# Prompt attention: VectorE makes sortable keys one beat later, and GpSimd takes the threshold step of each counting pass of the larger tiles

## What is computed

```python
def indexer_scores(iq, iw, ik):
    dots = jnp.einsum('nqhd,nsd->nqhs', iq, ik).astype(jnp.float32) * IDX_HEAD_DIM ** -0.5
    return jnp.einsum('nqh,nqhs->nqs', iw.astype(jnp.float32), jax.nn.relu(dots))
...
    def block(args):
        qb, iqb, iwb, qpos = args
        scores = indexer_scores(iqb, iwb, ik)
        scores = jnp.where((key_pos[None, :] <= qpos[:, None])[None], scores, -jnp.inf)
        _, idx = lax.top_k(scores, n_sel)
        valid = idx <= qpos[None, :, None]
        return selected_attention(qb, gather_rows(k, idx), gather_rows(v, idx), valid)
```

## Time and profile before

| what | value |
|---|---|
| median of three runs | 7764.09 us |
| profiled execution | 7772.33 us |
| span of its instructions | 7770.6 us |
| mean granted TensorE clock | 0.912 of full speed |
| PE busy over the span | 6543.4 us (84%) |
| DVE busy | 4540.9 us (58%) |
| ACT busy | 4234.9 us (54%) |
| POOL busy | 868.5 us (11%) |

### The profile page before, as it was taken

The page is one execution under the profiler, slowest core; times in us unless marked ns, Lnnn a source line. Parts: engine busy times, 40 slices in busy tenths (PEclk is TensorE's granted clock), DMA queues, the critical chain, the costliest instruction groups (busy, mean ns, idle before and its releaser), DMA issues. The chain is left out here.

```text
span 7770.6 us, 107932 instructions
## 1 busy us (share of the span) xinstructions
PE 6543.4 (84%) x37238; PEld 4012.5 (52%) x37238; DVE 4540.9 (58%) x12417; ACT 4234.9 (54%) x6108; POOL 868.5 (11%) x1398
## 2 busy tenths in 40 slices
PE   7999997888889998999989888847999469999970
PEld 2888884334444444444444444436455356666650
DVE  1555555777778877888888777853466400000017
ACT  1555553677778877888888887512333112221125
POOL 0111110000000000000000000000111233333335
PEclk9999998888989988999999999967999789999995
DMA  5121110000000000000000000023333168888888
GB/s 201 44 46 45 45 41 18 11 8 6 6 4 6 4 4 4 4 4 6 4 5 6 6 6 8 9 93 148 100 100 104 48 242 329 321 329 319 327 302 309
DMA packets 298319, 703.88 MB, mean 91 GB/s; under 512 B 120277, under 2 KB 166357, under 8 KB 257140
## 3 DMA queue, kind: packets, MB, share of 16 engines
q0 software_dynamic: 71520, 432.08, 15.0%
q1 hardware_dynamic: 225264, 257.29, 10.3%
q10 hardware_dynamic: 1094, 8.85, 0.3%
HBM read 559.43 MB, written 138.83 MB: 90 GB/s over the span
## 5 line engine op out<-in xcount | busy, mean ns | idle before, releaser
L818 ACT ACTIVATE at_junk<-at_key,at_thr 128x1024 int8<-128x1024 int16 (+56 forms) x858 | 1225.0, 1428 | 366.1 <-DVE at_thr L1061 322.3
L1018 DVE TENSOR_SCALAR_CACHE_REDUCE at_junk<-at_key,at_thr 128x384 int8<-128x384 f32 (+51 forms) x990 | 1301.8, 1315 | 46.1 <-issue 0.8
L906 PE MATMUL at_pS<-keep_KT,at_q 64*128 64x512 f32 (+3 forms) x2304 | 653.2, 645 | 200.9 <-DVE at_mx L1100 199.9
L1100 DVE CUSTOM_DVE_ANT_0 at_sm<-at_pS,at_drop 128x512 f32<-128x512 f32 (+3 forms) x1152 | 697.5, 643 | 87.5 <-PE at_pS L906 85.1
L937 PEld LDWEIGHTS at_pT<-keep_ident,at_sm 128*128 128x128 f32 x4224 | 505.7, 152 | 451.7 <-issue 433.0
L962 PE MATMUL at_pD<-keep_KT,keep_ident 128*128 128x512 f32 (+29 forms) x1602 | 653.5, 533 | 64.2 <-ACT at_relu L842 63.3
L917 PE MATMUL at_pD<-keep_IKT,at_iq 32*128 32x512 f32 (+3 forms) x2272 | 663.0, 662 | 35.4 <-ACT at_relu L842 34.3
L867 ACT ACTIVATE at_pt_sb<-at_pT 128x1024 f32<-128x1024 f32 (+3 forms) x576 | 546.1, 948 | 212.7 <-PE at_pT L937 211.7
L937 PE MATMUL at_pT<-keep_ident,at_sm 128*128 128x128 f32 x4224 | 641.1, 298 | 19.8 <-issue 11.5
L842 ACT ACTIVATE at_relu<-at_pD 128x1024 f32<-128x1024 f32 (+3 forms) x568 | 538.5, 948 | 203.2 <-PE at_pD L917 201.7
L2112 DVE TENSOR_TENSOR ex_gu<-ex_pg,ex_sg 128x256 f32<-128x256 f32 x98 | 41.6, 424 | 1003.3 <-ACT ex_sg L2094 1003.3
(11 more groups left out here) (432 smaller groups left out, 10134.9 us busy)
## 6 DMA issues: line engine op xcount, KB each, us to landing
scratch_ys<-ex_y SPq DMA_DIRECT2D x98, 512.0 KB, 2.7
scratch_x<-mx_x SPq DMA_DIRECT2D x33, 512.0 KB, 6.5
scratch_h<-mx_h SPq DMA_DIRECT2D x33, 512.0 KB, 2.6
cb_x<-scratch_x SPq DMA_DIRECT2D x33, 512.0 KB, 5.5
pj_x<-in_x_prompt SPq DMA_DIRECT2D x32, 512.0 KB, 3.6
mx_x<-in_x_prompt SPq DMA_DIRECT2D x32, 512.0 KB, 5.9
out_y_prompt<-cb_out SPq DMA_DIRECT2D x32, 512.0 KB, 4.6
scratch_qT<-pj_qT SPq DMA_DIRECT2D x33, 384.0 KB, 2.5
```

What stands on the lines that cost most here:

```text
L818: e.activation(junk[:, at], src[:, at], ACT.Sign, bias=bias, scale=-1.0, accum_out=cA[:, :]).then_inc(s["cnt"], 1)
L906: last = e.matmul(pS[:, kv, 0:w], Q[rows, t % 2, p, :], KT[rows, c * CUT:c * CUT + w], start=True, stop=True)
L1018: ch.then(e.tensor_scalar(junk[:, at], src[:, at], value, None, ALU.is_ge, ALU.add, accum_out=cD[:, :]))
L1100: e.tensor_tensor_reduce(sm[:, kv, at:at + w], pS[:, kv, 0:w], drop[:, t % 2, c * CUT:c * CUT + w], -HD ** -0.5, -NEG, ALU.add, ALU.min, m ...
```

## The change

Three things change in `phase_attend`.

1. `fresh_keys` is due one beat later than before, under the name `fresh`; ACT's `raw_scores` stays where it was.
2. For tiles with `CH(t) >= 4` (`guided`, L(t) from 1664 to 4096 keys: 20 tiles, 660 passes) the threshold step runs on GpSimd. DVE's count raises a semaphore `found`, ACT's count raises `cnt` as before, and GpSimd does kk, dlt and thr as three `tensor_scalar` instructions of 128x1 elements. kk is issued as soon as ACT's count is there, dlt waits for `found`. DVE goes from its count straight to the reads. The smaller tiles keep `decide` on DVE. `at_bigw` moves into the walk over the beats, at the end of the stage before.
3. The planner reckons 0.2 us instead of 0.7 us for a guided pass on DVE, and the load of the keys with `fresh`. This changes `splits`: over the 660 guided passes DVE counts 1,057,216 columns instead of 881,952, of 1,900,800. It changes `fills` too: over stages 8 to 27 from 201,265 to 161,427 columns.

```diff
+        guided = lambda t: CH(t) >= 4
+        found = lambda t, i: 33 * sum(guided(x) for x in range(2, t)) + i
+        needed = lambda t: sum(guided(x) for x in range(2, t + 1))
...
                 elif q == 0 and c > 0:
                     due(b, "wsum", (k, c - 1, 1))
                     due(b + 1, "raw", (k, c - 1))
+                    due(b + 2, "fresh", (k, c - 1))
...
+            if k + 1 < PT:
+                due(base + B - 1, "heads", k + 1)
...
-            v += 0.7 * len(passes)
+            v += sum(0.2 if guided(t) else 0.7 for t, i in passes)
...
+                def decide(t, i):
+                    n_act = L(t) - splits[t, i]
+                    e.wait_ge(s["cnt"], counted(t, i + 1 if i < 16 else i + 2))
+                    ch.ready()
...
+                    step = float(1 << (15 - i % 16))
+                    ch.link(e.tensor_scalar(kk[:, :], cA[:, :], 0.5, (2 * TOPK - 0.5 - n_act) / 2, ALU.mult, ALU.add))
+                    e.wait_ge(s["found"], found(t, i) + 1)
+                    ch.link(e.tensor_scalar(dlt[:, :], cD[:, :], kk[:, :], step, ALU.is_ge, ALU.mult))
+                    moved = e.tensor_scalar(thr[:, :], dlt[:, :], thr[:, :], -max(step / 2, 1.0), ALU.add, ALU.add)
+                    if i % 16 < 15:
+                        moved.then_inc(s["thr"], 1)
...
+                head_weights(2)
+                for beat in beats:
+                    for one in beat.get("heads", []):
+                        head_weights(one)
+                    for t, what, i in beat.get("find", []):
+                        if what == "pass" and guided(t):
+                            decide(t, i)
...
                 def count(t, i, src, value, n):
                     e.wait_ge(s["thr"], event(t, n))
                     ch.ready()
+                    wait(e, s["found"], found(t, i) if guided(t) else found(t, 0))
                     at = slice(0, splits[t, i])
-                    ch.then(e.tensor_scalar(junk[:, at], src[:, at], value, None, ALU.is_ge, ALU.add, accum_out=cD[:, :]))
+                    done = e.tensor_scalar(junk[:, at], src[:, at], value, None, ALU.is_ge, ALU.add, accum_out=cD[:, :])
+                    if guided(t):
+                        done.then_inc(s["found"], 1)
+                    else:
+                        ch.then(done)
...
                         if i == 0:
                             ch.ready()
                             wait(e, s["thr"], event(t, 0))
+                            wait(e, s["found"], found(t, 0))
+                            wait(e, s["cnt"], counted(t, 0))
+                            wait(e, s["needed"], needed(t - 1))
...
-                    for one in beat.get("raw", []):
+                    for one in beat.get("fresh", []):
                         fresh_keys(*one)
...
-                        early = what == "pass" and VECTOR * splits[t, i] > SCALAR * (L(t) - splits[t, i])
+                        early = what == "pass" and not guided(t) and VECTOR * splits[t, i] > SCALAR * (L(t) - splits[t, i])
...
-                        if what == "pass" and not early:
+                        if what == "pass" and not guided(t) and not early:
                             decide(t, i)
```

More of the change, by code:

```diff
@@ L657, in phase_attend @@
         pD = pb("at_pD", [P, 2, CUT]); pS = pb("at_pS", [P, NKV, CUT]); pT = pb("at_pT", [P, NKV, CUT]); pW = pb("at_pW", [P, CUT]); pO = pb("at_pO", [P, CUT])
-        names = "setup picked wm wcol wready iq0 iq1 q0 q1 bigw dot relu wsum wev thr cnt equal under kept qk ttr rowmax exp tr evac pv oev ot norm stored own".split()
+        names = "setup picked wm wcol wready iq0 iq1 q0 q1 bigw dot relu wsum wev thr cnt equal under kept qk ttr rowmax exp tr evac pv oev ot norm stored own found needed pool_own".split()
         s = {n: ctx.enter_context(phase_semaphore(nc, "at_" + n)) for n in names}
@@ L710, in phase_attend @@
                 due(base + B + 3, "raw", (k, CH(k) - 1))
+                due(base + B + 4, "fresh", (k, CH(k) - 1))
             if 2 <= k - 2 < PT:
@@ L738, in phase_attend @@
             v = sum(2 * (0.24 + VECTOR * width(t, c)) for t, p, c in beat.get("qk", []))
-            v += sum(0.3 + 1.5 * VECTOR * width(t, c) for t, c in beat.get("raw", [])) + 0.5 * len(beat.get("norm", [])) + 0.3 * len(beat.get("unload", []))
+            v += sum(0.3 + 1.5 * VECTOR * width(t, c) for t, c in beat.get("fresh", [])) + 0.5 * len(beat.get("norm", [])) + 0.3 * len(beat.get("unload", []))
             a = sum(0.12 + 2 * SCALAR * width(t, c) for t, c, q in beat.get("dot", [])) + sum(0.12 + 2 * SCALAR * width(t, c) for t, p, c in beat.get("evac", []))
@@ L801, in _, with head_weights @@
                 e.wait_ge(s["wready"], 1)
-                for t in range(2, PT):
+                ch = Chain(e, s["pool_own"])
+                def head_weights(t):
                     if t >= 4:
@@ L1086, in mask @@
                         ch.ready()
+                        wait(e, s["needed"], needed(t))
                         ch.then(e.scalar_tensor_tensor(mark[:, a:b], runs[:, a:b], need[:, :], mark[:, a:b], ALU.is_lt, ALU.mult))
```

15 lines of the change are left out of this document (added).

## The result

| what | before | changed |
|---|---|---|
| median | 7764.83 us (4 runs, 7754.96 to 7781.74) | 7558.12 us (4 runs, 7546.17 to 7565.88) |
| ratio | | 0.973, 95% interval 0.9708 to 0.9752 |
| span of the profiled execution | 7770.6 us | 7544.5 us |
| from the first pass of tile 7 to the first pass of tile 27 | 3033.0 us | 2830.6 us |

The changed kernel is 207 us faster. 150 us were forecast. Of the 226 us between the two profiled spans 202 lie in the search of the guided tiles. The attention as a whole (up to the first instruction of GpSimd in the phase behind it, 5105.7 and 4894.3 us) gives 211 us, and the remaining 15 us lie behind it, where nothing was changed.

What follows compares the result with a forecast made beforehand. The prediction held that no engine was full and DVE's lateness held up ACT and PE. Shorter queues -150, GpSimd step +20, tile boundaries +10, later keys -30 gave -150 us: 7614 us, range 7495 to 7755.

Runs made afterwards that it cites:

- wait_kept: The changed kernel, with DVE still waiting at the old place for ACT's copy of the raw scores, though it makes the keys a beat later: 7690.02 us, ratio 0.9907.
- one_more_link: The changed kernel with one more dependent instruction (times 1.0) in each threshold step on GpSimd: 7659.66 us, ratio 0.9865.

## What to carry to other kernels

In an in-order queue look at what stands behind a wait, not only at how long it is: if other engines wait for that work and it doesn't need the thing waited for, a large part of the wait is in the path of all of them (here 132 us of time for 275 us of waiting in wait_kept), and shortening the queue elsewhere makes that wait longer (here 191 to 274 us). Remove such a meeting point first, and move small work to another engine only afterwards, together with the balance that turns freed time into work. A serial step should go to the engine that is free only where something else covers it. Uncovered, it is sooner done on the engine that has just counted: 0.60 us on DVE here, 1.10 us on GpSimd where ACT's count ends last.

## What the runs showed of the hardware

- GpSimd's tensor_scalar of 128x1 takes 0.19 us (kk) to 0.22 us (the extra link of one_more_link) with constants only, and 0.30 us with a second operand read from SBUF; the next dependent one starts 0.08 to 0.10 us after its end.
- While DVE runs an instruction with two SBUF inputs, a GpSimd instruction that reads SBUF lasts until that has ended (2.14 us instead of 0.30; 125 of 125 cases in the changed kernel). Beside DVE's reads of logits (one input in PSUM, one in SBUF) and its counts (one input) it stays at 0.19 and 0.30 us.
- Granted clock in the guided stretch: 0.92 before (3034 us, PE idle 325 us) and 0.95 with late keys (2889 us, PE idle 250 us), with the same work on PE; 0.94 in the changed kernel (2831 us) and 0.96 with 25% more filling (2810 us).
